# Rounding the high halves of all weights in Pool's casting transfers, with a set of smaller reorderings, in an fp32 transformer kernel

## The chip, the cores and the metric

The kernel runs on one core of one Trainium2 chip. The time is the device time of the one program, in microseconds (us), the median of several executions.

## What is computed

The reference runs two blocks on 512 tokens of width 1024, in fp32, with 18 + 28 weight tensors. Cut to what matters:

```python
def first_block(x, ...):
    f = _swiglu(_rmsnorm(x, ffn1_pre_g), w_gate, w_up, w_down)      # 1024 -> 2816 -> 1024
    x = x + 0.5 * _rmsnorm(f, ffn1_post_g)
    qa, ka, va, qb, kb, vb, gate_a, gate_b = split(_rmsnorm(x, mix_pre_g) @ w_in)
    ya = _neighbourhood_attention(qa, ka, va, na_rpb) @ w_branch_a
    yb = _dilated_mixture(qb, kb, vb, slopes) @ w_branch_b
    x = x + _rmsnorm((sigmoid(gate_a) * ya + sigmoid(gate_b) * yb) @ w_out, mix_post_g)
    return x + 0.5 * _rmsnorm(_swiglu(...), ffn2_post_g)

def hybrid_layer(x, p_i, ...):                                      # twice
    z = rmsnorm(x, mix_norm) @ w_in
    o_a, o_b, o_c = nsa_attention(...), swa_sink_attention(...), mla_attention(...)
    g_a, g_b, g_c = split(sigmoid(h @ w_branch_gate))
    x = x + (g_a * (o_a @ w_a) + g_b * (o_b @ w_b) + g_c * (o_c @ w_c)) @ w_out
    x = x + (silu(h2 @ w_ffn_gate) * (h2 @ w_ffn_up)) @ w_ffn_down
    return x + sigmoid(rmsnorm(x, ple_norm) @ w_ple_gate) * (p_i @ w_ple_proj)
```

## The kernel before, in words

**Products in three parts.** A weight and an activation are each split in a high half, rounded to the short format of TensorE's fast fp32 mode (fp32r), and a low half, the rest. A product is three matmuls (`three`, lines 1716 to 1719): high by high, high by low, low by high, each 128 x 128 weights against 512 tokens.

**Units.** The weights come in 538 *units*, each a transfer of up to 128 x 1024 fp32 (512 KB) that serves 24 matmuls; those of the branches have 128 x 512 (256 KB, 12 matmuls) or 128 x 768. Three queues work through the same list of units, in order:
- SP (`weights`, line 2366) loads unit u into the raw buffer u % 3, once the halves of unit u - 3 are made;
- ScalarE (`halves`, line 1896) copies it with rounding into plane 0 of the split buffer u % 4 (L1903), once TensorE is through with unit u - 4;
- DVE (`rests`, line 2030) subtracts, raw less high, into plane 1 (L2036).

**Order of work.** A plan (`Plan`) is a list of steps, written by one Python program. Each engine walks through the whole list and runs its own part of a step (`tensor`, `scalar`, `vector`, `gpsimd`, `sync`), with semaphore waits where a step names an event. An engine's order is thus the order of the steps. A `dense` step of unit u carries `split_to=u + 2` and `load_to=u + 4`: at this step ScalarE and DVE make the halves up to unit u + 2 and SP issues the loads up to u + 4. At a `stream` step they go further ahead.

**Pool's part** is small: loads and stores of helper tensors (step `load`, L2342), sums of squares (`square`, L2346), a power for the reciprocal root (`var`, L2350), products with sines (`rope`, L2359). Those loads and stores wait in Pool's queue for their data:
- `bias_tables` (line 1006) in the first feed-forward part: a table goes to HBM and back twice, each transfer behind the landing of the one before;
- `tangent` (line 664): a gate's tanh is stored to HBM (`gate_scratch`) for later;
- `merge` (line 1045): for 24 products (three branches, eight blocks) in each of the last two layers, and 16 in the first block, `fetch(j + 3)` brings a gate back into a ring of four buffers. It waits until step `opened` of product j - 1 (L2191, and L2197 for all but the first branch) has used the buffer. Then comes `dense` of product j, then `opened` of j.

```python
        for j, (m0, n, m) in enumerate(order):
            fetch(j + 3)
            ...
            bo, bb, to = self.dense([(nm_, m, c0, ch) for nm_, c0, ch in parts], xs_)
```

**Output projections** `wo2` of the two layers (`residual`, line 1584; eight units each): after the product of block m DVE adds it to x (`plus`, L2323), ScalarE multiplies by the gain (L1929) and squares (L1933), Pool adds the square (L2346) for all blocks but the first.

**Start.** SP loads gains, x in eight parts and the first two units between them; ScalarE and DVE split x with the gain; `abreast` runs two units of the first feed-forward part, chunk by chunk of x.

## Time and profile before

| | us |
|---|---|
| median of 3 runs (3055.96 to 3058.5) | 3056.87 |
| the profiled execution | 3057.74 |
| its span, first to last instruction | 3055.6 |
| TensorE busy (matmuls) | 3013.4 |
| VectorE (DVE) busy | 1669.0 |
| ScalarE (ACT) busy | 1204.0 |
| GpSimd (Pool) busy | 289.1 |
| HBM read and written | 299.24 and 27.52 MB |

Busy time of an engine is the time in which it has an instruction; matmuls overlap, so that 0.39 us of one stand beside a step of 0.227 us from one to the next. The time given for a wait is that of an engine which had nothing else to do. "Landing" is the end of a transfer; the time to landing counts from its issue.

### The profile page before, as it was taken

The numbers are of one execution on the slowest core, as the hardware profiler recorded it, in microseconds if no ns is written. First come the engines' busy times: TensorE is split into PE (matmuls) and PEld (weight loads), VectorE is DVE, ScalarE is ACT, GpSimd is POOL, SyncE is SP. The second block draws the span as 40 slices with busy tenths as digits, with TensorE's granted clock in tenths as the row PEclk, the third lists the DMA queues.
The fourth block names the chain that finished last, engine by engine and source line by source line (L and its number), as shares of the span: only waits on it lengthen the run. The fifth ranks groups of instructions, "written<-read, shape, count | busy, mean of one in ns | idle before, by whom it ended". The sixth has DMA issues, their size and how long they took to land.

```text
span 3055.6 us, 40040 instructions
## 1 busy us (share of the span) xinstructions
PE 3013.4 (99%) x15272; PEld 2474.4 (81%) x15272; DVE 1669.0 (55%) x3050; ACT 1204.0 (39%) x2238; POOL 289.1 (9%) x344
## 2 busy tenths in 40 slices
PE   8999999999999999999999999999999999999998
...
GB/s 165 115 98 110 107 144 134 104 87 182 94 97 97 104 109 111 74 103 165 82 79 167 96 97 97 97 98 152 89 101 120 121 51 192 97 97 97 106 95 97
DMA packets 105996, 338.15 MB, mean 111 GB/s; under 512 B 15360, under 2 KB 15888, under 8 KB 105680
## 3 DMA queue, kind: packets, MB, share of 16 engines
q1 hardware_dynamic: 84816, 272.45, 28.5%
q0 software_dynamic: 20992, 63.15, 7.1%
...
HBM read 299.24 MB, written 27.52 MB: 107 GB/s over the span
## 4 chain that ended last, share of the span: by engine, by line
PE 91%; ACT 3%; DVE 2%; issue 2%; DMA 1%; POOL 1%; SPq 0%; POOLq 0%; DVEq 0%; ACTq 0%
PE bk L1717 26%; PE bk L1719 26%; PE bk L1718 26%; PE bk L1793 3%; PE bk L1815 3%; PE bk L1801 2%; PE bk L1756 1%; PE bk L1757 1%; PE bk L1758 1%; ACT t L1955 1%; DVE t L2036 0%; ACT t L1903 0%; PE bk L1769 0%; DMA t<-gate_scratch 0%; ACT t L1995 0%
## 5 line engine op out<-in xcount | busy, mean ns | idle before, releaser
L1717 PE MATMUL bk<-t,t 128*128 128x512 f32 x3784 | 1480.2, 391 | 19.6 <-DVE t L2036 14.6
L1719 PE MATMUL bk<-t,t 128*128 128x512 f32 x3784 | 1468.6, 388 | 0.0
L1718 PE MATMUL bk<-t,t 128*128 128x512 f32 x3784 | 1468.2, 388 | 0.0
L1717 PEld LDWEIGHTS bk<-t,t 128*128 128x128 f32 x3784 | 712.3, 188 | 175.6 <-issue 26.9
L1719 PEld LDWEIGHTS bk<-t,t 128*128 128x128 f32 x3784 | 712.4, 188 | 146.9
L1718 PEld LDWEIGHTS bk<-t,t 128*128 128x128 f32 x3784 | 712.7, 188 | 142.0
L2036 DVE TENSOR_TENSOR t<-t,t 128x1024 fp32r<-128x1024 f32 (+3 forms) x538 | 614.7, 1161 | 354.9 <-ACT t L1903 354.5
L1903 ACT CAST t<-t 128x1024 fp32r<-128x1024 f32 (+3 forms) x538 | 511.6, 979 | 229.8 <-PE bk L1719 119.5
L1946 ACT CAST t<-t 128x512 fp32r<-128x512 f32 x88 | 54.6, 621 | 433.8 <-DVE t L2096 433.8
L2346 POOL TENSOR_TENSOR t<-t,t 128x512 f32<-128x512 f32 x58 | 78.2, 1349 | 1387.3 <-ACT t L1933 1387.3
L1955 ACT ACTIVATE t<-t,t 128x256 f32<-128x256 f32 (+3 forms) x336 | 173.1, 517 | 75.8 <-DVE t L2109 75.0
L2093 DVE SCALAR_TENSOR_TENSOR t<-bk,t 128x512 f32<-128x512 f32 x88 | 60.5, 691 | 247.0 <-PE bk L1719 246.9
L2109 DVE CUSTOM_DVE_ANT_0 t<-bk,t 128x256 f32<-128x256 f32 (+3 forms) x272 | 110.0, 456 | 104.5 <-PE bk L1793 63.4
L1929 ACT ACTIVATE t<-t,t 128x512 fp32r<-128x512 f32 x72 | 51.0, 722 | 223.4 <-DVE t L2323 194.7
L1963 ACT COPY t<-bk 128x512 f32<-128x512 f32 (+2 forms) x200 | 96.7, 559 | 103.1 <-PE bk L1801 102.0
L1943 ACT ACTIVATE t<-t 128x512 f32<-128x512 f32 x88 | 55.5, 632 | 189.7 <-DVE t L2087 189.7
L1793 PE MATMUL bk<-t,t 64*128 64x256 f32 (+7 forms) x672 | 112.7, 414 | 3.2 <-ACT t L1963 2.6
L2342 POOL DMA_DIRECT2D gate_scratch<-t x64 | 35.3, 552 | 691.7 <-ACT t L1979 664.6
L1815 PEld LDWEIGHTS bk<-t,t 128*64 128x64 f32 x1456 | 78.8, 137 | 21.5 <-issue 20.8
L1801 PE MATMUL bk<-t,t 128*128 128x128 f32 x728 | 91.4, 273 | 4.2 <-DVE t L2241 1.5
L1801 PEld LDWEIGHTS bk<-t,t 128*128 128x128 f32 x728 | 82.0, 140 | 15.1 <-issue 3.2
L1793 PEld LDWEIGHTS bk<-t,t 64*128 64x128 f32 (+1 forms) x672 | 64.1, 187 | 35.2 <-ACT t L1963 22.0
...
## 6 DMA issues: line engine op xcount, KB each, us to landing
t<-in_f_g SPq DMA_DIRECT2D x88, 512.0 KB, 4.4
t<-in_f_u SPq DMA_DIRECT2D x88, 512.0 KB, 3.6
t<-in_f_d SPq DMA_DIRECT2D x64, 512.0 KB, 4.3
t<-in_gate SPq DMA_DIRECT2D x48, 512.0 KB, 3.7
gate_scratch<-t POOLq DMA_DIRECT2D x64, 256.0 KB, 2.4
t<-gate_scratch POOLq DMA_DIRECT2D x64, 256.0 KB, 3.9
...
t<-in_wo SPq DMA_DIRECT2D x24, 512.0 KB, 3.8
```

The source lines that it names most:

```text
L1717: pe.matmul(o, wh, xh, start=start, stop=False)
L1718: pe.matmul(o, wh, xl, start=False, stop=False)
L1719: return pe.matmul(o, wl, xh, start=False, stop=stop)
L1793: ins = pe.matmul(b["bank"][:, w["at"]:w["at"] + w["w"]], w["q"], w["k"], start=True, stop=True)
L1801: ins = pe.transpose(b["bank"][:, j * 128:(j + 1) * 128], b["S"][:, j * 128:(j + 1) * 128], P.cn("ident"))
L1815: ins = pe.matmul(v["o"], v["v"][j], b["PT"][:, c:c + 128], start=j == 0 and not v["add"], stop=end, skip_group_check=v["add"])
L1903: e.then_inc(act.copy(P.spl[u % NSPL][:, 0, 0:n], P.raw[u % NRAW][:, 0:n]), "halves", ("hi", u))
L1955: e.then_inc(act.activation(S, S, ACT.Exp, bias=w["nm"], scale=-1.0, accum_out=w["sm"]), "exps", (n, "e", j, i))
L1963: e.then_inc(act.copy(b["PT"][:, 0:b["w"]], b["bank"][:, 0:b["w"]]), "acts", (n, "a", j))
L2036: e.then_inc(dve.tensor_tensor(lo, P.raw[u % NRAW][:, 0:n], hi.bitcast(F32), ALU.subtract), "rests", ("lo", u))
L2109: e.then_inc(dve.tensor_tensor_reduce(b["S"][:, c:c + k], b["bank"][:, c:c + k], w["table"], -w["scale"], w["init"], ALU.add, ALU.min, w[" ...
L2346: e.then_inc(pool.tensor_tensor(P.acc[:], P.acc[:], s["q"][:], ALU.add), "pools", (n, "p"))
```

## The change

All edits are in one file.
1. **High halves.** `halves` leaves ScalarE for Pool. Pool issues, for each unit, a second transfer from HBM, from fp32 into the fp32r plane 0 of the split buffer, which rounds on the way. It waits until the products and the subtraction of unit u - 4 are done. It stands at the head of the same steps as ScalarE's copy did. DVE's subtraction waits for both landings (raw and high); SP waits for the subtraction alone.
2. **Start.** The first two units are cut in four of 256 KB (`cut=2`), the loads are spread among those of x (`START`), 12 products on a tile of ones run ahead, and the sums of squares of x come behind the first group of products.
3. **Last square.** The last of a row of squares isn't added; TensorE sums it as a second accumulation (`late`).
4. **`postnorm`.** The sum's products come before the first product of the embedding, the second product and its store after the factor.
5. **Gates.** The last gates of a stage are brought back two products earlier, in other buffers (`gate_back`, `there`).
6. Two copies of a query out of PSUM go to DVE in two places (`heads_in`), the turning of compressed scores takes banks of the other ring, two gates stream further ahead (`sooner`).

```diff
@@ -278,13 +279,16 @@
         self.stage()
         return b, bank, (n, "pe")
 
-    def abreast(self, names, xs):
+    def abreast(self, names, xs, cut=1):
         got = [self.OB.take() for _ in names]
         w = len(names)
-        us = [self.unit(name, m, 0, K, ahead=w - 1 - k) for k, (name, m) in enumerate(names)]
+        us = [[] for _ in names]
+        for p in range(cut):
+            for k, (name, m) in enumerate(names):
+                us[k].append(self.unit(name, m, p * (K // cut), K // cut, ahead=w * cut - 1 - p * w - k))
         order = [(c, k) for c in range(KC - 2) for k in range(w)] + [(c, k) for k in range(w) for c in (KC - 2, KC - 1)]
         n = self.step("abreast", banks=[g[1] for g in got], bts=[g[2] for g in got], us=us, order=order,
-                      xs=[xs(c) for c in range(KC)], load_to=us[-1][0] + 4, split_to=us[-1][0] + 2)
+                      xs=[xs(c) for c in range(KC)], load_to=us[-1][-1][0] + 4, split_to=us[-1][-1][0] + 2)
         self.stage()
         return [(g[0], g[1], (n, "pe", k)) for k, g in enumerate(got)]
 
...
@@ -315,6 +319,9 @@
             return (n, "a"), (n, "a")
         i, q, f = self.tmp.take()
         n = self.step("square", src=src, q=q, f=f, t=list(t), acc_t=self.acc_tok, on=on)
+        if on == "sums":
+            self.last_square = (i, q, (n, "a"))
+            return self.acc_tok, (n, "a")
         self.tmp.give(i, (n, "p"))
         return (n, "p"), (n, "a")
 
...
@@ -434,11 +444,9 @@
     def postnorm(self, gain, ft, xt, gi, product, store, n=4):
         first, second, got = self.rms(DM, self.acc_tok, self.rstd[:], self.vec_now())
         self.stream(4, on=("act",))
+        first()
         product(0)
-        first()
-        p1 = product(1)
         store(0)
-        store(1)
         self.stream(4, on=("dve",))
         k, spread = second()
         new, ht = [], []
...
@@ -450,6 +458,8 @@
 
         nxt = normed(0)
         self.steps[k]["behind"] = (nxt[2], "h")
+        p1 = product(1)
+        store(1)
         product(2)
         pt = product(3)
         for c in range(KC):
...
@@ -767,18 +781,21 @@
         self.c_tok = self.landing("c")
         self.step("begin")
         self.one_tok, self.half_tok, self.gh_tok = ("one", "half", "gh")
+        b, bank, _ = OB.take()
+        self.step("idle_products", bank=bank[:, 0:128])
+        OB.give(b)
 
         ht = []
         for c in range(KC):
             ht.append(self.gained(0, c, xt[c]))
-            if c < 2:
-                self.step("stream", load_to=-1, split_to=c, on=("act", "dve"))
-        for c in range(KC):
-            self.acc_tok, r = self.square_in(self.xT[:, c, :], c == 0, xt[c], on="dve")
-        self.factor()
-
-
-        xs = self.ffn("f1", ht, hook=self.rope_tables(), wide=1)
+            if c in START:
+                self.step("stream", load_to=-1, split_to=START[c], on=("act", "dve"))
+
+        def sums():
+            for c in range(KC):
+                self.acc_tok, r = self.square_in(self.xT[:, c, :], c == 0, xt[c], on="dve")
+            self.factor()
+        xs = self.ffn("f1", ht, hook=self.rope_tables(), wide=1, cut=2, then=sums)
         free = self.now()
         post, ft = self.add_post(free)
         fetch, halves, product, store = self.embed(0, 0, 40 * K, 32 * K, free)
...
@@ -1042,7 +1060,12 @@
             self.rope_tok.append(self.load(D["rope"][i], d[:], x))
             self.rope_done.append(self.rope_tok[-1])
 
-    def merge(self, mg, fr, branches, group, hooks=None, view=None):
+    def gate_back(self, name, m):
+        i, g, f = self.tmp.take()
+        at, stored = self.gate_at[name, m]
+        return self.tmp, i, g, self.load(g[:], self.D["gates"][at], f, stored)
+
+    def merge(self, mg, fr, branches, group, hooks=None, view=None, there=()):
 
         toks = [None] * KC
         back = Ring([self.tile([128, T], self.RA + (80 + 2 * i) * K) for i in range(4)])
...
@@ -1067,7 +1091,7 @@
                     fr = self.now()
             gname, g0, parts, xs_ = branches[n]
             bo, bb, to = self.dense([(nm_, m, c0, ch) for nm_, c0, ch in parts], xs_)
-            i, g, ld = got[j]
+            held, i, g, ld = got[j]
             if n == 0:
                 ia, s, f = self.tmp.take()
                 accs[m] = (ia, s)
...
@@ -1253,19 +1277,22 @@
                 b, bank, tok = res[2]
                 self.rope(bank, b, tok, [(pe[m // 2], 0, 128)], rt_[:, 2, :], rt_[:, 3, :], r_t[2:4], [fr, idle], later=later,
                           done=rotated)
-            if m % 2 == 0 and not later:
-                turning()
             got = []
             for R, (b, bank, tok) in ((kf, res[0]), (qf, res[1])):
                 took = [R[j].take() for j in range(2)]
                 w = []
-                for j in range(2):
+                if later and R is qf:
+                    k = self.step("rows", dst=[took[j][1][64 * j:64 * j + 64, :] for j in range(2)],
+                                  src=[bank[64 * j:64 * j + 64, :] for j in range(2)],
+                                  t=[tok, took[0][2], took[1][2], fr, idle])
+                    w = [(k, "d")] * 2
+                for j in range(2 - len(w)):
                     k = self.step("copied", dst=took[j][1][64 * j:64 * j + 64, :], src=bank[64 * j:64 * j + 64, :],
                                   t=[tok, took[j][2], fr, idle])
                     w.append((k, "a"))
                 PB.give(b, *w)
                 got.append((took, w))
-            if m % 2 == 0 and later:
+            if m % 2 == 0:
                 turning()
             tq = got[1][0]
             qt2 = []
...
@@ -1722,6 +1753,10 @@
         kind, n = s["kind"], s["n"]
         if kind == "here":
             e.here((n, "pe"))
+        elif kind == "idle_products":
+            e.wait_ge(P.one_tok)
+            for _ in range(12):
+                pe.matmul(s["bank"], P.ones[:], P.ones[:], start=True, stop=True)
         elif kind == "dense":
             e.wait_ge(s["bt"])
             for i, (u, tiles) in enumerate(s["parts"]):
...
@@ -1762,7 +1800,13 @@
                         e.then_inc(ins, "sums", (n, "pe", t))
         elif kind == "var":
             e.wait_ge(s["bt"], s["tok"], P.one_tok)
-            for k, accs in enumerate(s["accs"]):
+            if s["late"]:
+                for a, t in ((P.acc, None), s["late"]):
+                    e.wait_ge(t)
+                    for c in range(s["cols"]):
+                        ins = pe.matmul(s["bank"][:, c:c + 1], a[:, c * 128:(c + 1) * 128], P.ones[:, 0:1], start=t is None and c == 0,
+                                        stop=t is not None, skip_group_check=True)
+            for k, accs in enumerate(() if s["late"] else s["accs"]):
                 for c in range(s["cols"]):
                     for i, acc in enumerate(accs):
                         a = acc[:, c * 128:(c + 1) * 128] if c < 4 else acc[:, c - 4:c - 4 + 509:4]
...
@@ -1893,27 +1937,11 @@
 
     act = e.eng
 
-    def halves(s):
-        while e.parted <= min(s["split_to"], len(P.units) - 1):
-            u = e.parted
-            n = P.units[u][3]
-            e.wait_ge(("raw", u))
-            if u >= NSPL:
-                e.wait_ge(("used", u - NSPL))
-            e.then_inc(act.copy(P.spl[u % NSPL][:, 0, 0:n], P.raw[u % NRAW][:, 0:n]), "halves", ("hi", u))
-            e.parted += 1
-
     for s in P.steps:
         kind, n = s["kind"], s["n"]
         if kind == "here":
             e.here((n, "act"))
-        elif kind in ("dense", "abreast", "squeeze"):
-            halves(s)
-        elif kind == "stream":
-            if "act" in s["on"]:
-                halves(s)
         elif kind == "tokens":
-            halves(s)
             if s["ws"][-1]["k"] == s["nk"] - 1:
                 for t in range(4):
                     e.wait_ge((n, "pe", t), s["free"])
...
@@ -2031,7 +2059,7 @@
         while e.parted <= min(s["split_to"], len(P.units) - 1):
             u = e.parted
             n = P.units[u][3]
-            e.wait_ge(("hi", u))
+            e.wait_ge(("raw", u), ("hi", u))
             hi, lo = (P.spl[u % NSPL][:, p, 0:n] for p in range(2))
             e.then_inc(dve.tensor_tensor(lo, P.raw[u % NRAW][:, 0:n], hi.bitcast(F32), ALU.subtract), "rests", ("lo", u))
             e.parted += 1
...
@@ -2333,8 +2361,20 @@
 def gpsimd(e, P):
 
     pool = e.eng
+
+    def halves(s):
+        while e.parted <= min(s["split_to"], len(P.units) - 1):
+            u = e.parted
+            name, m, c0, n = P.units[u]
+            if u >= NSPL:
+                e.wait_ge(("used", u - NSPL), ("lo", u - NSPL))
+            pool.dma_start(P.spl[u % NSPL][:, 0, 0:n], P.D[name][m, :, c0:c0 + n]).then_inc(e.sems[f"u{u % NSPL}"], 16)
+            e.parted += 1
+
     for s in P.steps:
         kind, n = s["kind"], s["n"]
+        if kind in ("dense", "abreast", "squeeze", "tokens") or kind == "stream" and "act" in s["on"]:
+            halves(s)
         if kind == "here":
             e.here((n, "pool"))
         elif kind == "load":
...
@@ -2368,7 +2408,7 @@
             i = e.loaded
             name, m, c0, n = P.units[i]
             if i >= NRAW:
-                e.wait_ge(("hi", i - NRAW), ("lo", i - NRAW))
+                e.wait_ge(("lo", i - NRAW))
             sp.dma_start(P.raw[i % NRAW][:, 0:n], P.D[name][m, :, c0:c0 + n]).then_inc(e.sems[f"w{i % NRAW}"], 16)
             e.loaded += 1
 
...
@@ -2378,8 +2418,9 @@
             sp.dma_start(P.gn[:], P.D["gains"]).then_inc(e.sems["g"], 16)
             for c in range(KC):
                 sp.dma_start(P.xT[:, c, :], P.D["xT"][:, c, :]).then_inc(e.sems[f"x{c}"], 16)
-                if c < 2:
-                    weights(c)
+                if c in START:
+                    weights(START[c])
+            weights(4)
             sp.dma_start(P.con[:], P.D["const"]).then_inc(e.sems["c"], 16)
             sp.dma_start(P.gcn[:], P.D["cgains"]).then_inc(e.sems["c"], 16)
         elif "load_to" in s:
```

**Where the casts stand in Pool's order: the tables.** Pool's queue in the first feed-forward part, as it was (from the power for the first root, L2350, on). `t_81` takes the positions, `line_scratch` and `table_scratch` are the tables in HBM; the brackets name the semaphores waited for (`s_m2` and `s_m3` are landings).

```order
L2350 TENSOR_TENSOR t_66<-t_66 128x4 [waits s_vecs]
L2342 DMA t_81<-in_positions 128x512 [waits s_rests,s_acts,s_vecs,s_halves,s_pools,s_stats,s_sums]
L2342 DMA t_66<-in_rpb 128x31 [waits s_vecs]
L2342 DMA line_scratch<-t_66 2048x1x63 [waits s_m2]
L2342 DMA table_scratch<-line_scratch 16x128x32 [waits s_m3]
L2342 DMA table_scratch<-line_scratch 16x128x32 x2
```

And now. The casts (L2371) of four units stand ahead, the next behind the tables:

```order
L2390 TENSOR_TENSOR t_66<-t_66 128x4 [waits s_vecs]
L2371 DMA t_58<-in_f_u 128x1024 [waits s_rests,s_sums]
L2382 DMA t_81<-in_positions 128x512 [waits s_rests,s_vecs,s_acts,s_pools,s_stats,s_sums]
L2382 DMA t_66<-in_rpb 128x31 [waits s_vecs]
L2382 DMA line_scratch<-t_66 2048x1x63 [waits s_m2]
L2382 DMA table_scratch<-line_scratch 16x128x32 [waits s_m3]
L2382 DMA table_scratch<-line_scratch 16x128x32 x2
L2371 DMA t_55<-in_f_g 128x1024
L2371 DMA t_56<-in_f_u 128x1024
```

What moved: the casts for hidden block 3 (`t_55<-in_f_g`, `t_56<-in_f_u`) and all that follow stand behind two waits for landings.

**The merge of a layer.** Pool's queue, as it was: one fetch of a gate (L2342) after another, each behind DVE's use of the buffer (`s_vecs`).

```order
L2342 DMA t_166<-gate_scratch 128x512 [waits s_vecs]
L2342 DMA t_167<-gate_scratch 128x512 [waits s_vecs]
L2342 DMA t_168<-gate_scratch 128x512 [waits s_vecs,s_m9]
L2342 DMA t_169<-gate_scratch 128x512 [waits s_vecs,s_m10]
L2342 DMA t_166<-gate_scratch 128x512 [waits s_vecs,s_m11]
```

And now, with the fetches at L2382 and the casts of branch weights (`in_br2a`, `in_br2c`, `in_br2b`) at L2371:

```order
L2382 DMA t_166<-gate_scratch 128x512 [waits s_vecs]
L2371 DMA t_58<-in_br2a 128x512 [waits s_sums]
L2382 DMA t_167<-gate_scratch 128x512 [waits s_vecs,s_m10]
L2371 DMA t_55<-in_br2c 128x512 [waits s_rests,s_sums]
L2382 DMA t_168<-gate_scratch 128x512 [waits s_vecs,s_m11]
L2371 DMA t_56<-in_br2c 128x512 [waits s_rests,s_sums]
L2382 DMA t_169<-gate_scratch 128x512 [waits s_vecs,s_m0]
L2371 DMA t_57<-in_br2b 128x512 [waits s_rests,s_sums]
```

What moved: each cast stands behind a fetch, and each fetch behind a use by DVE. DVE's queue at the same place now: L2064 is the subtraction, which waits for the cast (`s_u0` to `s_u3`) and the raw load (`s_w0` to `s_w2`); L2219 and L2225 are the product with the gate and the sum (`opened`).

```order
L2064 TENSOR_TENSOR t_55<-t_53,t_55 128x512 [waits s_u0,s_w1]
L2219 SCALAR_TENSOR_TENSOR t_71<-t_168,bk 128x512 [waits s_sums,s_m3]
L2064 TENSOR_TENSOR t_56<-t_54,t_56 128x512 [waits s_u1,s_w2]
L2219 SCALAR_TENSOR_TENSOR t_72<-t_169,bk 128x512 [waits s_sums,s_m4]
L2064 TENSOR_TENSOR t_57<-t_52,t_57 128x512 [waits s_u2,s_w0]
L2219 SCALAR_TENSOR_TENSOR t_166<-t_166,bk 128x512 [waits s_sums,s_m5]
L2225 TENSOR_TENSOR t_71<-t_71,t_166 128x512 [waits s_vecs]
L2064 TENSOR_TENSOR t_58<-t_53,t_58 128x512 [waits s_u3,s_w1]
L2219 SCALAR_TENSOR_TENSOR t_167<-t_167,bk 128x512 [waits s_sums,s_m6]
L2225 TENSOR_TENSOR t_72<-t_72,t_167 128x512 [waits s_vecs]
```

In DVE's queue nothing moved but what the subtraction waits for.

**An output projection.** Pool's queue now: a sum of squares (L2386) stands between the casts of `in_wo`; before, only the sums stood there.

```order
L2371 DMA t_55<-in_wo 128x1024 [waits s_rests,s_sums]
L2371 DMA t_56<-in_wo 128x1024 [waits s_rests,s_sums]
L2386 TENSOR_TENSOR t_64<-t_64,t_68 128x512 [waits s_acts]
L2371 DMA t_57<-in_wo 128x1024 [waits s_rests,s_sums]
L2386 TENSOR_TENSOR t_64<-t_64,t_69 128x512 [waits s_pools,s_acts]
L2371 DMA t_58<-in_wo 128x1024 [waits s_rests,s_sums]
L2386 TENSOR_TENSOR t_64<-t_64,t_70 128x512 [waits s_pools,s_acts]
```

The cast for the unit two ahead stands behind the sum of the block before.

## Rows read from the trace of the kernel before

**Rows 1.** The page: busy time of engines; the chain that ended last.

```profile
PE 3013.4 (99%) x15272; PEld 2474.4 (81%) x15272; DVE 1669.0 (55%) x3050; ACT 1204.0 (39%) x2238; POOL 289.1 (9%) x344
PE 91%; ACT 3%; DVE 2%; issue 2%; DMA 1%; POOL 1%; SPq 0%; POOLq 0%; DVEq 0%; ACTq 0%
```

**Rows 2.** Waits of TensorE: who for whom, us in total, times, longest.

```profile
PE bk L1717 <- DVE t L2036: 14.6, 11, 8.8
PE bk L1717 <- ACT t L1995: 3.6, 2, 1.8
```

**Rows 3.** Timeline of TensorE at the start: start us, us, engine, line.

```profile
8.80 0.76 PE L1717 MATMUL bk<-t,t 128*128 128x512 f32 x1 [8.80 <-DVE t L2036]
11.66 0.77 PE L1717 MATMUL bk<-t,t 128*128 128x512 f32 x1 [1.25 <-DVE t L2036]
```

**Rows 4.** DMA queues (packets, MB, share of 16 engines); issues, KB, us to landing.

```profile
q1 hardware_dynamic: 84816, 272.45, 28.5%
q0 software_dynamic: 20992, 63.15, 7.1%
t<-in_f_g SPq DMA_DIRECT2D x88, 512.0 KB, 4.4
t<-value_scratch POOLq DMA_DIRECT2D x2, 512.0 KB, 3.9
```

**Rows 5.** Groups of instructions, 62 to 270 us: busy, mean ns, idle before.

```profile
L2036 DVE TENSOR_TENSOR t<-t,t 128x1024 fp32r<-128x1024 f32 x38 | 44.9, 1220 | 4.5 <-ACT t L1903 4.5
L1903 ACT CAST t<-t 128x1024 fp32r<-128x1024 f32 x37 | 37.1, 1046 | 1.7 <-PE bk L1719 1.7
```

**Rows 6.** Timelines of Pool, 40 to 62 us, and of TensorE at 47 us.

```profile
40.97 0.72 POOL L2342 DMA_DIRECT2D t<-in_positions  x1 [14.03 <-DVE t L2144]
47.98 1.15 POOL L2342 DMA_DIRECT2D line_scratch<-t  x1 [5.75 <-DMA t<-in_rpb]
58.63 3.14 POOL L2342 DMA_DIRECT2D table_scratch<-line_scratch  x3 [9.50 <-DMA line_scratch<-t]
...
46.73 0.39 PE L1719 MATMUL bk<-t,t 128*128 128x512 f32 x1
46.96 0.39 PE L1717 MATMUL bk<-t,t 128*128 128x512 f32 x1
```

**Rows 7.** A merge: DMA issues, 1594 to 1664 us; timelines of DVE and Pool.

```profile
t<-gate_scratch POOLq DMA_DIRECT2D x20, 256.0 KB, 3.7
...
1615.88 0.69 DVE L2197 TENSOR_TENSOR t<-t,t 128x512 f32<-128x512 f32 x1
1620.60 0.68 DVE L2036 TENSOR_TENSOR t<-t,t 128x512 fp32r<-128x512 f32 x1
1621.20 0.68 DVE L2191 SCALAR_TENSOR_TENSOR t<-t,bk 128x512 f32<-128x512 f32 x1
...
1617.11 0.54 POOL L2342 DMA_DIRECT2D t<-gate_scratch  x1 [2.19 <-DVE t L2197]
```

**Rows 8.** An output projection: timelines of DVE, ScalarE and Pool.

```profile
1680.41 0.69 DVE L2323 TENSOR_TENSOR t<-t,bk 128x512 f32<-128x512 f32 x1 [0.97 <-PE bk L1719]
1683.35 1.53 DVE L2036 TENSOR_TENSOR t<-t,t 128x1024 fp32r<-128x1024 f32 x1 [0.71 <-ACT t L1903]
...
1681.13 0.73 ACT L1929 ACTIVATE t<-t,t 128x512 fp32r<-128x512 f32 x1 [3.25 <-DVE t L2323]
1681.76 0.62 ACT L1933 ACTIVATE t<-t 128x512 f32<-128x512 f32 x1
...
1682.45 1.34 POOL L2346 TENSOR_TENSOR t<-t,t 128x512 f32<-128x512 f32 x1 [4.10 <-ACT t L1933]
```

**Rows 9.** Timeline of Pool at three other places.

```profile
451.10 5.58 POOL L2342 DMA_DIRECT2D t<-value_scratch  x8 [4.99 <-DMA value_scratch<-t]
...
1192.80 2.14 POOL L2342 DMA_DIRECT2D t<-rope_scratch  x4 [21.46 <-PE bk L1719]
...
1409.42 0.56 POOL L2342 DMA_DIRECT2D gate_scratch<-t  x1 [3.48 <-ACT t L1979]
```

60 lines of the change are left out of this document (39 added, 21 removed).

## Prediction

> **What bounds the kernel now.** I read the page first: TensorE is busy 3013.4 of 3055.6 us, the chain that ended last runs over it for 91%, and Pool is busy 9% [rows 1]. So a change gains only where TensorE stands idle, and loses wherever it makes TensorE wait. Then the waits of TensorE: the largest is 14.6 us for the low halves (L2036), then 3.6 us for copies out of PSUM [rows 2]; all of them make some 33 us, the start included. Then the start: the first matmul begins at 8.80 us, the next group at 11.66 us [rows 3]. Then the supply of weights, which the change rebuilds. Loads of weights hold the 16 DMA engines 28.5% of the span, Pool's transfers 7.1% [rows 4]. In a feed-forward stretch DVE's subtractions take 1.220 us each and wait 4.5 us in total for ScalarE in 208 us [rows 5]: the supply runs ahead, by about two units of 24 x 0.227 = 5.45 us. Note that 0.227 us is the step between two matmuls (46.96 less 46.73 us) [rows 6].
>
> **What the casts change.** A rounding that ScalarE did in about 1.05 us, on data already in SBUF, becomes a transfer of its own. It has two prices. First, latency: issue to landing of a load from Pool's queue is 3.7 us for 256 KB [rows 7] and 3.9 us for 512 KB [rows 4]; I take 4.1 us for 512 KB, since a raw load of that size, which took 4.4 us, now runs beside it. The rate with a cast stands in no row; I take the plain one, with half of it as the other bound. Second, order: Pool works through its queue in order, so a cast starts only after the Pool instruction ahead of it, and DVE, which subtracts right after, holds its own queue until the landing.
>
> The Trainium skill (DMA: Bandwidth & Descriptors, Anatomy of one DMA — SWDGE path) gives 2.0 us plus bytes by 436 GB/s, so 2.6 us for 256 KB and 3.2 us for 512 KB; by it the loops below would be 1.1 and 0.9 us shorter, and the result about 3285 us. The rows are measured under this kernel's traffic and stand.
>
> Traffic: 272 MB more at the same rate adds 28.5% to 35.9%, 64%. No bound by itself. In the feed-forward stretches Pool has nothing to wait for: a cast starts when the slot four units back is free, that is three units (16 us) before it is needed, and takes 0.6 + 4.1 + 1.2 us. Margin 10 us, cost nothing. The cover is those three units. In attention a unit lasts 10 to 20 us, since it is used in quarters; cost nothing either.
>
> **Where it costs**, place by place.
> 1. *Tables.* Pool issues positions at 40.97 us, then waits 5.75 us and 9.50 us for landings and ends the last table transfer at 61.77 us. The cast for the unit that TensorE starts at 46.96 us now stands behind that: 61.77 + 0.6 + 4.1 + 1.2 = 67.7, 20.7 us late [rows 6]. I take +20.
> 2. *The merges of the two last layers.* Per unit (12 matmuls, 2.72 us) Pool fetches a gate, then casts. The fetch waits for DVE to have consumed a gate; DVE does that behind a subtraction that waits for the cast before. That closes a ring of one turn per unit. From the rows: subtraction to product 0.60 us (1620.60 to 1621.20), to sum 0.72, sum to fetch 1.23 (1615.88 to 1617.11), fetch 0.54, cast to landing 3.7, wake 0.1: 6.9 us; without the sum (a third of the units) 6.2 [rows 7]. On average 6.65 against 2.72 us, 18 turns: +71, and some 4 us on entering, where the fetches wait for everything before. Two layers: +150.
> 3. *The first merge.* Ten turns, half of 6.2 and half (384 KB) of 7.3 us, against 34 us: +33; +35 with the entry.
> 4. *Output projections of the two layers* (L2323 and what follows). Here a ring runs through DVE's addition (0.72 us to the gain), the gain (0.63), the square (0.69 to Pool), Pool's sum 1.34, the cast 4.1, wake 0.1 and the subtraction 1.53: 9.1 us per unit against 5.45 [rows 8]. Seven turns of 3.65 us, less 2 us of margin at first: +23 each, +46.
> 5. *Single waits.* Eight loads of values wait 4.99 us and end at 456.7 us, +5; the rope tables at 1192.80 us hold Pool while the subtraction is due at once, +10; between the compression products a cast follows a gate store that waits for its tanh at 1409.42 us, for six or so units per layer by 2 to 4 us each, +15 a layer, +30 [rows 9]. Bounds for these three together 15 and 75 us.
> 6. *Restarts.* A matmul at the start took 0.76 us where 0.39 is usual [rows 3, 6]; after long gaps I add 5 us in all.
>
> **The other edits.** Earlier and smaller first units, x spread among the loads, 12 idle products, sums after the first group: the start now moves 1 MB of raw halves and 1 MB of casts besides x, so only part of the 8.80 + 1.25 us is won; -3 (0 to -6). Late squares, the product moved behind the normalizing, two copies of a query given to DVE, prefetched gates: they aim at the 3.6 us, at part of the 14.6 us [rows 2] and at the smaller waits in the 33 us; -8 (0 to -14). The time that ScalarE saves is off the path: it ended no wait of TensorE there.
>
> Sum: 20 + 150 + 35 + 46 + 45 + 5 - 3 - 8 = +290 us. The profiled execution took 3057.7 us around its span of 3055.6, 0.9 over the median of 3056.87. So 3347; I say **3350 us**.
>
> **Rivals.**
> - *Queue alone* (12%): the rings don't close, because DVE meets landings that are already there; only Pool's lateness counts. Then in the merges a cast starts about 2.5 us after the end of the unit three back and is ready at 2.5 + 3.7 + 0.8 = 7.0, against 5.44: 1.6 us in part of 64 units, and nothing in 4. With 1 and 5 that is about +130: 3180 us. Against it: a subtraction stands ahead of each product in DVE's order.
> - *Slow casts* (15%): at half the rate a 256 KB cast needs 0.85 us more and a 512 KB one 1.7 us: 46 turns and 14 turns make +63, the single places +20: 3430 us. At a quarter of the rate 512 KB occupy the engines 7 us of every 5.45 us, and some 450 units lose 1.5 us or more: over 4000 us (5% of the 15).
> - *Hidden* (6%), the other side: Pool stands ahead of TensorE everywhere, as in the feed-forward stretches, and the other edits show: 3057 - 11 = 3046 us. It holds wherever Pool's instruction ahead of a cast is done by the time the slot comes free; it turns in the merges when landing plus 3.2 us exceeds 2.72 us, and in 4 when landing plus 5 exceeds 5.45. No row has a landing that short.
> - *Not what it says* (2%): where the rounding is made changes nothing, since the subtraction waits for a transfer as long as before; about 3055 us. The 4.5 us of [rows 5] speak against it: before, it hardly waited.
>
> **Numbers.** The forecast has 65%. Low end: queue alone with the ends of 5, 3190 us. High end: half rate with the upper ends of 5, 3520 us. This leaves out the hidden case, the quarter rate and part of the queue case, not quite 2 in 10. Faster by over 0.2% (6 us, what three runs of this kernel tell apart) 0.06, within it 0.01, slower 0.93.
>
> **What would show it.** Right if TensorE's waits for L2064 (the subtraction's new line) grow to about 290 us and lie in 45 to 70, 690 to 760 and in the two merges and output projections; if DVE's waits for the landing of casts replace those for ScalarE; if a unit in a merge takes 6 to 7 us; and if feed-forward stretches keep 0.227 us a matmul. Wrong if the merges keep under 4 us a unit (queue alone or hidden), or if feed-forward stretches slow down (slow casts).

## The result and the profile after

The changed kernel takes 3482.9 us (median of four runs, 3472.01 to 3486.42) against 3057.1 for the kernel before on the same chip: a ratio of 1.139, 95% interval 1.136 to 1.141, or 426 us more. The forecast was 3350, the range 3190 to 3520. The profiled execution took 3472.01 us around a span of 3470.2, which is 414.6 us more than the 3055.6 of before.

The page of the changed kernel: busy time of the engines, DMA queues (packets, MB, share of 16 engines), and two of the costliest groups (busy us, mean ns, idle before):

```profile
PE 3137.7 (90%) x15328; PEld 2545.8 (73%) x15328; DVE 1662.0 (48%) x3056; ACT 717.4 (21%) x1692; POOL 572.1 (16%) x884
q0 software_dynamic: 98752, 323.17, 31.0%
q1 hardware_dynamic: 85104, 272.45, 24.7%
L1748 PE MATMUL bk<-t,t 128*128 128x512 f32 x3784 | 1524.1, 403 | 259.8 <-DVE t L2064 238.1
L2064 DVE TENSOR_TENSOR t<-t,t 128x1024 fp32r<-128x1024 f32 (+3 forms) x540 | 615.3, 1145 | 990.9 <-DMA t<-in_f_d 241.7
```

ScalarE lost some 490 us of work and Pool gained some 280, and neither shows in the time; TensorE's share fell from 99% [rows 1] to 90%. Its waits, over the whole span (who for whom, us in total, times, longest), stand beside the 14.6 and 3.6 us of [rows 2]:

```profile
PE bk L1748 <- DVE t L2064: 238.1, 82, 20.8
```

Eighty-two waits for the low halves, and behind them DVE's waits for the landing of casts. (The prediction had looked for some 290 us on this line; another 21.8 us stand under the name of L2104, a DVE addition that is held by such a subtraction, see e12.) Traffic is not the matter: Pool's queue moved 260 MB more and its share grew from 7.1% of 3055.6 us [rows 4] to 31.0% of 3470.2, that is by 859 us of 16 engines' time, 303 GB/s; the raw loads made 272.45 MB in 24.7%, 318 GB/s. **A cast runs at nearly the plain rate.** (This takes all that Pool's share grew by as the casts'.)

Where the 415 us lie: for each weight unit I took the start of its first matmul in both traces; what a stretch grew by is the difference over it. In us, with the terms of the prediction and the experiments below (one profile each; the 5 us of the prediction's step 6 stand in no row):

| stretch (times of before) | predicted | changed | e1 | e4 | e6 | e7 | e9 |
|---|---|---|---|---|---|---|---|
| first gate and up products, with the tables (25-254) | +20 | 31.8 | 2.2 | 31.6 | 32.7 | 17.3 | 16.9 |
| normalizing behind the first feed-forward (382-422) | 0 | 16.2 | 0.2 | 15.2 | 16.7 | 16.9 | 15.1 |
| value loads (444-451) | +5 | 22.9 | 0.0 | 22.1 | 22.7 | 0.0 | 0.0 |
| attention behind them (451-684) | 0 | 5.0 | 0.0 | 4.1 | 3.9 | 21.4 | 22.6 |
| first merge (684-747) | +35 | 36.8 | -0.4 | 3.8 | 9.4 | 0.1 | 0.2 |
| merges of the two layers | +150 | 132.5 | -1.7 | -0.9 | 31.8 | 1.3 | -0.7 |
| three output projections and the entries behind them | +46 (two) | 46.0 | -0.3 | 47.3 | 7.2 | 49.7 | 6.5 |
| entry of the two layers, rope tables | +10 | 22.0 | -0.1 | 22.1 | 22.0 | 5.0 | 3.4 |
| compression products, two layers | +30 | 58.9 | -1.0 | 60.6 | 63.3 | 35.4 | 31.8 |
| per-layer embedding products, two layers | 0 | 20.9 | 0.0 | 21.9 | 21.8 | 9.3 | 9.2 |
| the rest | -8 | 22.2 | -8.4 | 19.6 | 30.2 | 21.7 | 26.7 |
| start (before the third unit) | -3 | -0.8 | -5.7 | -0.9 | -1.0 | -0.8 | -0.7 |

**The tables' stop** came as worked out. Pool, timeline 45 to 76 us (start us, us, engine, line; in brackets the idle time before and what ended it):

```profile
45.86 0.55 POOL L2382 DMA_DIRECT2D t<-in_positions  x1 [12.55 <-DVE t L2172]
49.69 1.15 POOL L2382 DMA_DIRECT2D line_scratch<-t  x1 [2.73 <-DMA t<-in_rpb]
59.02 3.15 POOL L2382 DMA_DIRECT2D table_scratch<-line_scratch  x3 [8.18 <-DMA line_scratch<-t]
62.16 0.58 POOL L2371 DMA_DIRECT2D t<-in_f_g  x1
```

The cast goes out at 62.16 us, behind the same three steps as in [rows 6], and TensorE waits 20.8 us, the longest wait in the row above. This stop is 22.8 of the 31.8 us. Another 6.9 come at a second stop that the prediction did not have: Pool waits for ScalarE before it stores the rope tables, with the casts of the next units behind that (timeline of Pool, 76 to 200 us).

```profile
162.98 0.55 POOL L2382 DMA_DIRECT2D rope_scratch<-t  x1 [14.81 <-ACT t L2016]
```

The last 2 us of this row are not the casts': e1, without casts, has 2.2 there.

**A merge** is the ring that was foreseen. Timeline of DVE, Pool and TensorE in the first of the two layer merges, one turn and the start of the next:

```profile
1828.20 0.69 DVE L2064 TENSOR_TENSOR t<-t,t 128x512 fp32r<-128x512 f32 x1 [2.72 <-DMA t<-in_br2c]
1828.81 0.68 DVE L2219 SCALAR_TENSOR_TENSOR t<-t,bk 128x512 f32<-128x512 f32 x1
1829.04 0.47 PE L1748 MATMUL bk<-t,t 128*128 128x512 f32 x1 [1.58 <-DVE t L2064]
1829.52 0.69 DVE L2225 TENSOR_TENSOR t<-t,t 128x512 f32<-128x512 f32 x1
1830.75 0.55 POOL L2382 DMA_DIRECT2D t<-gate_scratch  x1 [5.04 <-DVE t L2225]
1831.29 0.55 POOL L2371 DMA_DIRECT2D t<-in_br2b  x1
1834.45 0.69 DVE L2064 TENSOR_TENSOR t<-t,t 128x512 fp32r<-128x512 f32 x1 [2.85 <-DMA t<-in_br2b]
```

Subtraction, product, sum, fetch, cast, landing, subtraction: 6.25 us, every link as in [rows 7] but the last. From the cast's issue at 1831.29 to the subtraction it is 3.16 us, where the 3.7 us of the gate loads had been taken; the median landing of these casts over the stretch 1759 to 1891 us is 3.0 to 3.2 us (DMA issues: count, KB each, median us to landing):

```profile
t<-in_br2b POOLq DMA_DIRECT2D x8, 256.0 KB, 3.1
t<-in_br2a POOLq DMA_DIRECT2D x8, 256.0 KB, 3.2
t<-in_br2c POOLq DMA_DIRECT2D x6, 256.0 KB, 3.0
```

The Trainium skill (DMA: Bandwidth & Descriptors, Anatomy of one DMA — SWDGE path) gives 2.6 us for this size; the measurement lies between its fit and the rows of before.

**An output projection** is the longer ring. Timeline of ScalarE, DVE and Pool:

```profile
1910.73 0.68 DVE L2351 TENSOR_TENSOR t<-t,bk 128x512 f32<-128x512 f32 x1
1911.44 0.73 ACT L1957 ACTIVATE t<-t,t 128x512 fp32r<-128x512 f32 x1 [6.85 <-DVE t L2351]
1912.08 0.62 ACT L1961 ACTIVATE t<-t 128x512 f32<-128x512 f32 x1
1912.78 1.33 POOL L2386 TENSOR_TENSOR t<-t,t 128x512 f32<-128x512 f32 x1 [6.25 <-ACT t L1961]
1914.06 0.57 POOL L2371 DMA_DIRECT2D t<-in_wo  x1
1917.81 1.23 DVE L2064 TENSOR_TENSOR t<-t,t 128x1024 fp32r<-128x1024 f32 x1 [4.85 <-DMA t<-in_wo]
1918.95 0.68 DVE L2351 TENSOR_TENSOR t<-t,bk 128x512 f32<-128x512 f32 x1
```

Addition, gain, square, Pool's sum, cast, landing, subtraction, addition: 8.22 us, where 9.1 had been worked out from [rows 8] and the unit takes 5.45. TensorE first uses up its lead: the eight units of this projection take 5.4 us four times, then 5.9, 8.0, 8.1 and 8.2, and the two units behind them 13.0 and 7.8 where they took 6.3 and 5.9. So half of the ring's price is paid at the entry to the feed-forward part.

### The profile page after: what moved, and what is told of

Read it like the earlier page. It is cut to its first block, busy times and chain, and to the rows that moved or that the text cites. A ratio compares the mean times of both kernels' runs of the same rounds, so it can differ in the third digit from the quotient of the medians.

```text
span 3470.2 us, 40208 instructions
## 1 busy us (share of the span) xinstructions
PE 3137.7 (90%) x15328; PEld 2545.8 (73%) x15328; DVE 1662.0 (48%) x3056; ACT 717.4 (21%) x1692; POOL 572.1 (16%) x884
## 3 DMA queue, kind: packets, MB, share of 16 engines
q1 hardware_dynamic: 85104, 272.45, 24.7%
## 4 chain that ended last, share of the span: by engine, by line
PE 49%; DMA 9%; issue 8%; DVE 5%; POOL 3%; ACT 2%; POOLq 0%; DVEq 0%; SPq 0%; ACTq 0%
PE bk L1748 14%; PE bk L1749 14%; PE bk L1750 14%; PE bk L1837 2%; PE bk L1859 2%; PE bk L1845 1%; DMA t<-in_br2b 1%; DMA t<-in_br2a 1%; DMA t<-in_gate 1%; POOL t L2382 1%; DMA t<-in_br2c 1%; DVE t L2064 1%; DMA t<-in_plg 1%; DMA t<-in_cw 1%; DVE t L2219 1%
## 5 line engine op out<-in xcount | busy, mean ns | idle before, releaser
L1748 PE MATMUL bk<-t,t 128*128 128x512 f32 x3784 | 1524.1, 403 | 259.8 <-DVE t L2064 238.1
L1749 PE MATMUL bk<-t,t 128*128 128x512 f32 x3784 | 1503.3, 397 | 0.0
L1750 PE MATMUL bk<-t,t 128*128 128x512 f32 x3784 | 1501.8, 397 | 0.0
L2064 DVE TENSOR_TENSOR t<-t,t 128x1024 fp32r<-128x1024 f32 (+3 forms) x540 | 615.3, 1145 | 990.9 <-DMA t<-in_f_d 241.7
L1748 PEld LDWEIGHTS bk<-t,t 128*128 128x128 f32 x3784 | 732.8, 194 | 453.4 <-issue 276.1
L1750 PEld LDWEIGHTS bk<-t,t 128*128 128x128 f32 x3784 | 732.2, 194 | 155.4
L2121 DVE SCALAR_TENSOR_TENSOR t<-bk,t 128x512 f32<-128x512 f32 x88 | 60.6, 691 | 238.7 <-PE bk L1750 238.4
L2386 POOL TENSOR_TENSOR t<-t,t 128x512 f32<-128x512 f32 x58 | 79.3, 1368 | 448.7 <-ACT t L1961 448.7
L1837 PE MATMUL bk<-t,t 64*128 64x256 f32 (+7 forms) x672 | 116.1, 423 | 31.7 <-DVE t L2104 21.8
L2382 POOL DMA_DIRECT2D gate_scratch<-t x64 | 35.6, 556 | 630.7 <-ACT t L2007 602.0
L2371 POOL DMA_DIRECT2D t<-in_f_g x89 | 48.2, 541 | 395.8 <-PE bk L1750 259.5
L1837 PEld LDWEIGHTS bk<-t,t 64*128 64x128 f32 (+1 forms) x672 | 65.5, 191 | 65.1 <-DVE t L2104 22.9
L2371 POOL DMA_DIRECT2D t<-in_f_u x89 | 48.0, 539 | 354.8 <-PE bk L1750 343.2
```

What stands on the lines that cost most here:

```text
L1748: pe.matmul(o, wh, xh, start=start, stop=False)
L1749: pe.matmul(o, wh, xl, start=False, stop=False)
L1750: return pe.matmul(o, wl, xh, start=False, stop=stop)
L1837: ins = pe.matmul(b["bank"][:, w["at"]:w["at"] + w["w"]], w["q"], w["k"], start=True, stop=True)
L2064: e.then_inc(dve.tensor_tensor(lo, P.raw[u % NRAW][:, 0:n], hi.bitcast(F32), ALU.subtract), "rests", ("lo", u))
L2371: pool.dma_start(P.spl[u % NSPL][:, 0, 0:n], P.D[name][m, :, c0:c0 + n]).then_inc(e.sems[f"u{u % NSPL}"], 16)
```

## Experiments

All runs are set against the kernel before on the same chip (3057.0 to 3057.4 us). Where one run stands, it is worth some 7 us either way (the changed kernel's own four runs span 14); the growth of a stretch that an edit doesn't touch repeats better: the first layer merge grew by 66.0, 66.8, 67.3 and 66.5 us in four kernels that have it unchanged (the changed kernel, e11, e12, e10).

### e1: ScalarE's copies back, the rest kept

```diff
+def cast(P, u):
+    return False
...
+            if not cast(P, u):
...
+                e.then_inc(act.copy(P.spl[u % NSPL][:, 0, 0:n], P.raw[u % NRAW][:, 0:n]), "halves", ("hi", u))
```

ScalarE copies every unit for which `cast` is false, and Pool issues a cast only where it is true.

> The changed kernel with one thing undone: the high halves are ScalarE's copies again, Pool issues no casts; the other edits stay. Theory (the whole loss comes from the casts, and the other edits gain the 11 us of the prediction): 3046 us, between 3037 and 3056, and TensorE's waits below 33 us. Rival (some of the other edits cost time of their own, such as Pool's prefetched gates or the product moved behind the normalizing): more than 3065 us.

3043.48 us (five runs, 3041.53 to 3044.47), ratio 0.9956, interval 0.9942 to 0.9969. The whole loss is the casts'; the other edits gain 14 us (in the table's one profile 15: 5.7 at the start and 8.4 in the rest among them). **This version beats both kernels.**

### e2: the casts alone

The kernel before with the places of the diff that move the rounding, and nothing else.

> The kernel before with the casts alone, none of the other edits. Theory (the edits are apart from the casts): about 11 us above the changed kernel's 3483, so 3485 to 3505 us. Rival (an edit such as two normalizing squares summed late or the product moved behind the normalizing makes some of the single waits longer, because casts now stand behind it on Pool's queue): below 3470 us, with the missing part in the stretches from the end of a feed-forward layer to the next products. Second rival (the edits are what keeps the casts this cheap): above 3520 us.

3512.08 us, 7 above the expected span's upper end: with casts the other edits are worth 29 us in place of 14. It lies between the theory (to 3505) and the second rival (from 3520), and one run's 7 us don't decide between them. By stretches it is the merges (47.9, 74.9 and 76.5 us against 36.8, 66.0 and 66.5) and the compression (72.7 against 58.9). For the merges the likely reason is that gates fetched early spare the ring its entry; no run takes that edit alone.

### e3: casts in the feed-forward layers alone

```diff
+def cast(P, u):
+    return P.units[u][0][0] == "f"
```

with a cast on Pool where it is true, a copy on ScalarE where not.

> The changed kernel with casts only for the weights of the four feed-forward layers (352 of 538 units, some two thirds of the bytes), ScalarE's copies for all others. Theory (what costs is the place in Pool's queue and not the traffic or the rate of a cast): the kernel of e1 plus the tables at the start (+32 us as the changed kernel shows in that stretch) and some 5 to 15 us at entering the feed-forward layers, so about 3085 us, 3075 to 3105. Rival (each cast costs by its bytes): two thirds of the loss, 3046 + 290 = about 3335 us.

3101.87 us (3099.67 to 3102.67), ratio 1.0145, interval 1.0131 to 1.0159: 58 us over e1 as against 439 for all casts. (The counts in the expectation are wrong: it is 274 of the 540 units, about half, and the three merges have 64; the rival for half would have been some 3260.) Of the 58 us 30.6 lie in the tables' stretch, 22 at the output projections and the entries behind them, 5.4 at the start, and the remaining feed-forward products stay within 1 to 2 us a layer. Their matmuls, 1000 to 1100 us:

```profile
L1752 PE MATMUL bk<-t,t 128*128 128x512 f32 x148 | 57.6, 389 | 0.0
L2085 DVE TENSOR_TENSOR t<-t,t 128x1024 fp32r<-128x1024 f32 (+1 forms) x18 | 21.5, 1193 | 9.4 <-DMA t<-in_f_d 8.6 <-DMA t<-in_f_u 0.5
```

DVE does wait for landings (9.4 us in 100), TensorE doesn't (0.0). Half of all bytes cost next to nothing where Pool is free.

### e4: no casts in the merges

The same function with `P.units[u][0][:2] != "br"`.

> The changed kernel with ScalarE's copies for the weights of the three merges alone (88 units), casts elsewhere. Theory (the ring fetch, cast, landing, subtraction, product costs the 169 us by which the three merges grew): 3483 - 169 = 3314 us, 3300 to 3330, and a unit in a merge takes 2.7 to 3 us again. Rival (Pool's queue is late in the merges anyway, and the lateness only moves behind them, to the output projections): above 3350 us, with the stretch of the output projections longer than in the changed kernel.

3304.36 us, 10 below the expected sum. The merges grow by 3.8, -0.9 (both layers together), and nothing moves behind them: the output projections stay at 47.3 us. The parts add up.

### e5: the fetch behind the cast

```diff
-            fetch(j + 3)
             if hooks:
...
             bo, bb, to = self.dense([(nm_, m, c0, ch) for nm_, c0, ch in parts], xs_)
+            fetch(j + 3)
```

> The changed kernel with one line moved in the merges: a gate is fetched behind the products of its turn and no longer ahead of them, so on Pool's queue the cast stands ahead of the fetch that waits, and a product on DVE is followed by a cast that its next but one needs. Same instructions, same waits, same bytes. Theory (a ring of one turn per unit, 6.1 us by the changed kernel's trace): the ring now closes over two units, so 3.1 to 3.4 us per unit, each of the two layer merges grows by 10 to 20 us in place of 66, the first by 10 to 25 in place of 37; the sum about 3375 us, 3350 to 3400. Rival (no ring; a cast is simply slower than a unit of 2.72 us, its landing of 3 us or the rate being what the merges wait for): the period stays at 5 us or more, the time within 20 us of 3483.

3353.69 us: one moved line gives 129 us back. The layer merges grow by 17.0 and 16.9 us, the first by 9.0, and a unit takes 83.4 / 24 = 3.5 us, a little over the forecast band. Subtractions now come in pairs (timeline of DVE, a layer merge of this kernel):

```profile
1766.77 0.69 DVE L2064 TENSOR_TENSOR t<-t,t 128x512 fp32r<-128x512 f32 x1 [4.01 <-DMA t<-in_br2a]
...
1768.70 0.68 DVE L2064 TENSOR_TENSOR t<-t,t 128x512 fp32r<-128x512 f32 x1
...
1774.82 0.69 DVE L2064 TENSOR_TENSOR t<-t,t 128x512 fp32r<-128x512 f32 x1 [4.11 <-DMA t<-in_br2c]
```

Bytes, casts and waits are the same; what changed is over how many units the ring closes. That settles ring against rate.

### e6: Pool one unit further ahead

```diff
+        if kind == "dense" and s["parts"][0][0] is not None and P.units[s["parts"][0][0]][0][:2] in ("br", "wo"):
+            halves({"split_to": s["split_to"] + 1})
```

> The changed kernel, with Pool issuing in merges and output projections the cast of one unit further ahead (three where it was two), DVE's order unchanged. Theory (rings): the merges as in the run before, 3.1 to 3.4 us a unit, and the three output projections, which grew by 26 us, give back 10 to 20 of it, since their ring (addition, gain, square, Pool's sum, cast, subtraction) also closes over two units; the sum 3335 to 3390 us. Rival (the slot, not the queue, holds the cast: one unit further it waits for the matmuls of the unit before and blocks Pool meanwhile): merges better than 6.1 us but above 4 us a unit, output projections the same or longer, the sum above 3420 us.

3318.48 us, 17 below the expected span. The merges as in e5, and the output projections with their entries fall from 46.0 to 7.2 us, twice what was expected. (The 26 us in the expectation left out the entries behind them, 19.8 us, which went to 1.8.) Their ring, through Pool's sum, is as real as that of the merges.

### e7: plain loads and stores on SyncE

```diff
-            pool.dma_start(s["dst"], s["src"]).then_inc(e.sems[s["sem"]], 16)
+            sp.dma_start(s["dst"], s["src"]).then_inc(e.sems[s["sem"]], 16)
```

for all loads whose tiles are not float32r (those stay with Pool, and get semaphores of their own).

> The changed kernel with all of Pool's plain loads and stores (gates, tables, embeddings, values, rope tables) issued by SyncE, so that Pool's queue holds casts and Pool's own arithmetic only; raw loads now stand behind those waits instead, but with three raw buffers. Theory (place in Pool's queue is the price): merges near their old length (3 to 4 us a unit), the tables' stretch and the value loads below 10 us each; the single waits that go through Pool's sums and powers (output projections, normalizing) stay, 60 to 110 us in all; the sum 3130 to 3220 us. Rival (the waits move to the raw loads, which the same subtraction needs): above 3350 us, with DVE's waits for raw landings in place of casts.

3235.3 us, 15 above the band: 248 of the 426 us go once the plain loads and stores no longer stand between the casts. (The edit also gives these loads another kind of queue, and no run takes that apart. For the order speaks that in e5 and e6, which leave them on Pool, the layer merges give back three quarters as well.) Merges grow by 1.4 us in all. The tables' stretch keeps 17.3 us: its raw loads now stand behind the table steps. And the wait at the value loads only moves: from 22.9 us there to 21.4 in the attention, since three raw loads behind the eight loads of values now land after 13.4 us. TensorE's waits, 430 to 560 us:

```profile
PE bk L1850 <- DVE t L2219: 18.8, 2, 18.2
PE bk L1753 <- DVE t L2069: 14.0, 1, 14.0
```

### e8: idle products in the layer merges

```diff
+        elif kind == "warm":
+            for _ in range(8):
+                pe.matmul(s["bank"], P.ones[:], P.ones[:], start=True, stop=True)
```

> The changed kernel with 8 idle products (128 columns, results unused) behind each unit's matmuls in the two layer merges, 384 in all, 0.2 us each at full clock and 0.4 at half, 1.6 to 3.1 us a unit in a turn that has 3.4 us of idle time. Theory (the ring doesn't pass through TensorE; its clock is lost only where matmuls are on the path, in the stretches behind the rings and after single waits): merges keep 6.1 us a unit, their granted clock rises from 0.84 to above 0.95, the output projections behind them get at most 3 us shorter each, the sum 3473 to 3490 us. Rival (half clock in the rings is a cost on the path): the merges get shorter by 10 us or more each. Second rival (the ring passes through TensorE): each turn grows by 1.6 us or more, 75 us in all.

3491.74 us, 2 over the expected span, the merges 67.4 and 69.4 us where they were 66.0 and 66.5. The granted clock is the last number but two; the changed kernel's first layer merge and this one's:

```profile
1759.20:1891.50 132.30, 87.40 (x290) 64.51 (x289) 46.32 (x70) 5.63 (x9) 25.99 (x48) 0.85 0.51 154
```

```profile
1768.60:1902.40 133.80, 114.40 (x675) 99.25 (x673) 48.79 (x73) 5.64 (x9) 26.54 (x49) 0.99 0.52 157
```

The clock rose from 0.85 to 0.99 and nothing got faster, in the merges or behind them (9.6 and 9.8 us against 8.4 and 10.4). The ring doesn't pass through TensorE; the lower clock lay within its idle time.

### e9: e7 and e6 together

> The kernel of e7 (plain loads and stores on SyncE) with Pool one unit further ahead in merges and output projections, as in e6. Theory (what e7 left in the output projections and at entering the feed-forward layers behind them, some 45 us, is the ring through Pool's sums, which e6 opened): 3235 less 35 to 45, so about 3195 us, 3185 to 3210; the rest (about 130 us over e1's 3043) is single waits: the tables, the normalizing, the compression, value loads that now hold the raw loads. Rival (the two remedies take from the same waits): above 3220 us.

3188.02 us; the projections fall to 6.5 us, the merges to nothing. 145 us over e1 remain, in single places.

### e10: idle products ahead of the stops

```diff
+    def fill(u, bank):
+        for _ in range(FILL.get(u, 0)):
+            pe.matmul(bank[:, 0:128], P.ones[:, 0:bank.shape[0]], P.ones[:], start=True, stop=True)
```

> The changed kernel with idle products (128 columns, results overwritten) ahead of 21 of the units outside the merges for which TensorE waits, as many as fill the wait that the changed kernel's trace shows there less 0.3 us, at 0.22 us each (93 before the tables' unit, 64 before the first products behind the normalizing, 3 to 31 elsewhere, 362 in all). They move no wait, but hold the clock up. Theory (after a stop of 2 to 20 us some 8 to 15 matmuls run at the lower of the two clocks and cost 1.5 to 3 us each time, in all some 40 us outside the merges, of which these stops carry some 24): 3483 less 15 to 25, so about 3463 us, 3455 to 3470. Rival (the slow matmuls are covered by the next wait, or the fill itself comes too late and delays the unit): 3475 us or more.

3479.21 us (four runs, 3476.17 to 3485.31), ratio 1.1384, interval 1.1365 to 1.1403: no difference from 1.1387 that can be measured. **My theory fell.** The fill raised the clock as it should: matmuls of the three products (L1748 to L1750) that start more than 0.33 and under 0.9 us behind the one before them, outside the merges, fell from 252 to 158, and what they take beyond 0.227 us from 50 to 31 us (15 in the kernel before). The time didn't follow. In the tables' stretch 4.6 us came back (27.2 against 31.8); elsewhere the matmuls that ended sooner seem to have met their next wait sooner, which the trace allows but no run isolates. Nor is the rival's second half excluded: at nine of the 21 places the unit starts within 0.03 us of the last idle product, so the fill may have delayed it there.

### e11: the bias tables' bytes in long rows

```diff
-                          D["tables"][:, :, :, 7 - r:15 - r, :].rearrange("c w h a k -> c (w h) (a k)"), self.tables_t, ft[7])
+                          bass.AP(D["f1_g"].tensor, 6144 * r, [[6144 * 8, 16], [256, 24], [1, 256]]), self.tables_t, ft[7])
```

> The changed kernel with the eight loads of the bias tables (8 x 384 KB, rows of 1 KB, on Pool's queue before the first normalizing) reading the same bytes from a weight tensor in rows of 24 KB, so that the attention of the first branch gets other biases (its values are not the reference's); queue, order and bytes as they were. In the changed kernel they hold the 16 DMA engines at 99% for 30 us at some 110 GB/s, and three casts issued behind them land after 16.7 us. Theory (the 16 us by which that stretch grew are the landing of casts beside these short rows, not Pool's order): casts land within 8 us, the stretch grows by less than 6 us, the sum 3466 to 3476 us. Rival (Pool's order or the normalizing's own chain through Pool's power): growth stays at 14 to 17 us although the casts land sooner. Second rival (the 16 partitions that they write are what makes them slow, not the rows): DMA rate and landing stay as they were.

The attention of the first branch has other biases here. 3472.46 us, which is in the expected span, but within a single run's spread; the stretch decides, and it grew by 13.5 us in place of 16.2, not by less than 6. DMA issues of 410 to 460 us, in the changed kernel:

```profile
t<-table_scratch POOLq DMA_DIRECT2D x8, 384.0 KB, 17.2
t<-in_qka POOLq DMA_DIRECT2D x3, 512.0 KB, 16.7
t<-in_va SPq DMA_DIRECT2D x3, 512.0 KB, 5.5
```

This is how busy the 16 engines were in the same 50 us of the changed kernel (tenths in 40 slices, 9 is 90% or more, and GB/s):

```profile
DMA  8887657799999999999999999999999996887750
GB/s 177 341 223 285 243 200 226 177 105 95 131 95 105 125 102 105 125 98 111 121 102 111 121 98 125 115 102 125 105 108 193 400 410 190 216 298 256 229 233 7
```

and the issues of e11:

```profile
t<-in_f_g POOLq DMA_DIRECT2D x8, 384.0 KB, 16.3
t<-in_qka POOLq DMA_DIRECT2D x3, 512.0 KB, 12.9
```

The second rival comes nearer: with long rows the eight transfers still take 16.3 us, and the casts behind them 12.9, so the rows are worth 3 to 4 us of landing and 2.7 us of the stretch. In e7 the table loads had left Pool's queue, and yet three casts took 17.4 us in that stretch and it grew by 16.9. So it is mainly neither the row length nor the queue; that 16 partitions are all these loads write is the candidate left, and it wasn't tried. Nor is it Pool's order. The first of the three casts goes out when TensorE has freed its slot (Pool, changed kernel):

```profile
433.29 0.58 POOL L2371 DMA_DIRECT2D t<-in_qka  x1 [11.03 <-PE bk L1750]
```

It could not start sooner with four split buffers, so its landing is the whole price there; before, the raw load had landed by then and ScalarE's copy took 1 us. The Trainium skill (DMA: Bandwidth & Descriptors, SWDGE vs HWDGE vs iDMA) says that the two kinds of queues feed different internal queues of each engine, which takes turns between them; this trace shows no turns, but e7's 17.4 us show how little another queue helps here.

### e12: casts ahead of the value loads

```diff
+                self.step("stream", load_to=-1, split_to=len(self.units) + 3, on=("act",))
                 vst = self.load(D["values"].rearrange("(t p) c -> p t c", p=128), vn[:], v_n)
```

> The changed kernel with the casts of the next two gate units issued ahead of the value store and the eight value loads on Pool's queue (one step more in the plan, no instruction more). Theory (the 22.9 us by which that stretch grew come from a subtraction that stands on DVE's queue ahead of the attention's additions, and waits for a cast that Pool issues behind the value loads at 505 us and that lands 14.6 us later): the cast lands before 502 us, the wait of TensorE for L2104 falls from 21.8 to below 6 us, the sum 3460 to 3472 us. Rival (the attention waits for its values and tables anyway, which the same DMA engines bring): growth stays above 15 us with the wait under another name.

3465.64 us, within the expected span. The changed kernel, DVE at 519 us, and then TensorE's waits of 470 to 530 us in this one:

```profile
519.36 1.23 DVE L2064 TENSOR_TENSOR t<-t,t 128x1024 fp32r<-128x1024 f32 x1 [28.16 <-DMA t<-in_ga]
520.50 0.68 DVE L2104 TENSOR_TENSOR t<-bk,t 128x512 f32<-128x512 f32 x1
```

```profile
PE bk L1846 <- DVE t L2215: 9.3, 2, 8.7
```

In the changed kernel the matmuls that the attention's addition (L2104) waits for end at 499.5 us; it then stands 21 us behind a subtraction, for whose cast DVE is idle 28 us in all, and TensorE waits 21.8 us for it. With the cast sooner that stretch grows by 0.0 in place of 22.9 us, and L2104 holds nothing up. 9.8 us come back in the attention behind. That is not the rival's wait for the values: L1846 transposes the attention's probabilities into a PSUM bank that a gate's product (L2215) has to free first, and this product stands behind the next subtraction, whose cast was issued at 508.95 us, behind the value loads:

```profile
524.62 1.23 DVE L2065 TENSOR_TENSOR t<-t,t 128x1024 fp32r<-128x1024 f32 x1 [17.37 <-DMA t<-in_ga]
```

The values are first used at 533.0 us, without a wait for them. So the theory holds and its mechanism shows again one cast further on; 13 us were gained in the two stretches.

## Why the prediction was right or wrong

- **Right: the mechanism and its largest terms.** Rings in merges and projections, casts stuck behind Pool's steps at the tables. e5 and e6 show the rings by opening them.
- **Right in part by luck: the sum of these terms,** 251 us forecast and 247 measured. The layer merges were put 17 us too high (step 2: landing 3.7 us taken, 3.0 to 3.2 measured). The two projections of step 4 were put at 46 us and gave 36.6 with their entries (ring of 8.2 us in place of 9.1); the projection of the first block, which step 4 left out, gave the missing 9.4 at its entry. The tables' stretch was put 12 us too low, mostly for its second stop.
- **Luck: the range.** Its upper end, 3520 us, was "half rate with the upper ends of 5". A cast at half rate is not what happened, and the terms given make 3430 + 30 = 3460 us, under the measured 3482.9; 60 us of that end have no source. The lower end, 3190, doesn't come out of its terms either (3180 with the ends of step 5 is 3150 to 3210).
- **Right: feed-forward products cost nothing** (1.8 and 0.1 us in the down products; e3), and the rate is the plain one, so "slow casts" falls. "Queue alone" falls by the 6.25 us turn, "hidden" and "not what it says" by the sign.
- **Wrong: step 5, the single waits.** 45 us forecast, with 75 as the upper bound; measured 103.8: values 22.9, rope tables and entry 22.0, compression 58.9. Three things failed in that step. First, the landing of 4.1 us used everywhere: behind eight value loads three casts took 14.6 us, behind the bias tables 16.7 (both in the changed kernel), in the compression of the first of the two layers 5.6 to 6.1. The trace of before had the warning: in the first two places its raw loads, from another queue, took 11.0 and 13.4 us, hidden by a cover that the casts don't have. At the values this is some 10 of the 18 us that were missing. Second, what Pool waits for: at the values also 11.4 us for ScalarE ahead of the store, and in the compression (first layer; no run tests this reading) 27.2 us for three stores of gates and 18.5 us for three swapped rows (below). Third, the rope tables were counted for one layer: 10 us forecast, 10.2 measured there and 11.9 at the second.

```profile
POOL gate_scratch L2382 <- ACT t L2007: 27.2, 3, 10.5
POOL t L2399 <- DMA t<-t: 18.5, 3, 11.6
```

- **Wrong: places given as free.** Normalizing 16.2, the attention 5.0, the embedding products 20.9 and the rest 22.2 us: 64 us. At the normalizing the cast goes out in time and its landing beside the bias tables is the price (e11); the attention's 5.0 and the rest were not taken apart; between the embedding products Pool has fetches and sums of its own, which no run isolates. I had looked for Pool's waits that I knew, not gone through every stretch for a step of Pool between casts or a slow landing.
- **Step 6, the clock.** Given 5 us. Busy time of TensorE grew by 124 us, which looks like the missing part and, as far as the runs show, isn't: in the merges it lies inside the ring (e8), elsewhere taking half of what the slow steps cost away changed the time by nothing that can be measured (e10).
- **The other edits** were put at -11 us; alone they make -14 (e1), and beside the casts -29 (e2 against the changed kernel).
- The shortfall, then: single waits 59, places given as free 64, tables 12, other edits' 11 that don't show as a gain in the table, less 16 for the rings and 5 for the clock: 125 of the 125 us between 290 and 415. The median lies another 11 us above the profiled execution.
